# Gated-conv / GLA hybrid step: the small levels' scores in blocks of 32 tokens on the diagonal

## The reference, cut to what matters

```python
def gla_chunk(s, inp):
    q, k, v, gk = inp
    c = q.shape[2]
    b = jnp.cumsum(gk, axis=2)
    causal = jnp.tril(jnp.ones((c, c), dtype=bool))
    diff = b[:, :, :, None, :] - b[:, :, None, :, :]
    decay = jnp.exp(jnp.where(causal[None, None, :, :, None], diff, -jnp.inf))
    a = jnp.einsum('nhtd,nhsd,nhtsd->nhts', q, k, decay)
    o = jnp.einsum('nhts,nhsv->nhtv', a, v) + jnp.einsum('nhtd,nhdv->nhtv', q * jnp.exp(b), s)
```

## Time and profile before

| | us |
|---|---|
| median of 3 executions (lowest, highest) | 1970.84 (1970.3, 1971.75) |
| the profiled execution, device time | 1971.51 |
| its span, first to last instruction | 1969.7 |
| TensorE matmul busy | 1928.7 (98%) |
| TensorE weight load busy | 1863.0 |
| VectorE busy | 1086.9 |
| ScalarE busy | 814.3 |
| GpSimd busy | 360.0 |
| mean granted TensorE clock | 0.994 |

### The profile page before, as it was taken

How to read it: one execution, slowest core, us unless ns; L and a number is a source line. 1 busy time by engine, 2 the same in 40 slices (tenths; PEclk the granted TensorE clock), 3 DMA queues, 4 the chain that set the end, 5 groups by cost and what they waited for, 6 DMA issues and landing times. The chain is left out here.

```text
span 1969.7 us, 35737 instructions
## 1 busy us (share of the span) xinstructions
PE 1928.7 (98%) x14212; PEld 1863.0 (95%) x14212; DVE 1086.9 (55%) x1171; ACT 814.3 (41%) x1033; POOL 360.0 (18%) x423
## 2 busy tenths in 40 slices
PE   6999999999999999999999899999999999999997
PEld 5999889998899988999889899999999999999996
DVE  6556555565555655556565675444544454445555
ACT  5534445434454344543543353333333333333331
POOL 4241212312023120321200151000100010001400
PEclk9999999999999999999999899999999999999998
DMA  6645665557654476545744545555555555555542
GB/s 183 186 143 154 215 214 152 148 144 232 204 151 149 140 242 196 153 141 149 235 165 157 145 139 168 163 168 163 163 167 169 160 166 167 168 161 169 164 158 80
DMA packets 176152, 329.42 MB, mean 167 GB/s; under 512 B 11060, under 2 KB 29792, under 8 KB 175880
## 3 DMA queue, kind: packets, MB, share of 16 engines
q1 hardware_dynamic: 161016, 291.21, 49.4%
q10 hardware_dynamic: 9968, 19.16, 2.8%
q0 software_dynamic: 5072, 17.69, 2.8%
HBM read 306.59 MB, written 21.38 MB: 167 GB/s over the span
## 5 line engine op out<-in xcount | busy, mean ns | idle before, releaser
L351 DVE TENSOR_TENSOR w_lo<-raw,w_hi 128x1024 fp32r<-128x1024 f32 x544 | 724.4, 1335 | 798.0 <-ACT w_hi L346 797.8
L346 ACT ACTIVATE w_hi<-raw 128x1024 fp32r<-128x1024 f32 x544 | 574.7, 1058 | 919.0 <-PE bank L373 907.2
L371 PE MATMUL bank<-x_hi,w_hi 128*128 128x288 f32 (+2 forms) x3072 | 916.3, 298 | 5.1 <-DVE x_lo L397 2.9
L372 PE MATMUL bank<-x_lo,w_hi 128*128 128x288 f32 (+2 forms) x3072 | 910.7, 296 | 0.0
L373 PE MATMUL bank<-x_hi,w_lo 128*128 128x288 f32 (+2 forms) x3072 | 908.1, 296 | 0.0
L371 PEld LDWEIGHTS bank<-x_hi,w_hi 128*128 128x128 f32 x3072 | 578.0, 188 | 15.8 <-issue 11.2
L372 PEld LDWEIGHTS bank<-x_lo,w_hi 128*128 128x128 f32 x3072 | 578.1, 188 | 4.2 <-issue 2.9
L373 PEld LDWEIGHTS bank<-x_hi,w_lo 128*128 128x128 f32 x3072 | 577.4, 188 | 0.0
L373 PE MATMUL bank<-f_hi,w_lo 128*128 128x288 f32 x1280 | 379.5, 296 | 0.0
L371 PE MATMUL bank<-f_hi,w_hi 128*128 128x288 f32 x1280 | 378.9, 296 | 0.0
L372 PE MATMUL bank<-f_lo,w_hi 128*128 128x288 f32 x1280 | 373.2, 292 | 0.0
(11 more groups left out here) (238 smaller groups left out, 1044.1 us busy)
## 6 DMA issues: line engine op xcount, KB each, us to landing
raw<-in_w SPq DMA_DIRECT2D x256, 512.0 KB, 3.7
raw<-in_w_in SPq DMA_DIRECT2D x224, 512.0 KB, 3.7
out<-S ACTq DMA_DIRECT2D x36, 512.0 KB, 4.7
raw<-in_w_in SPq DMA_DIRECT2D x64, 256.0 KB, 3.1
S<-in_state_gla POOLq DMA_DIRECT2D x32, 512.0 KB, 6.6
raw<-in_w_o SPq DMA_DIRECT2D x32, 512.0 KB, 3.6
out<-yrow SPq DMA_DIRECT2D x8, 192.0 KB, 2.5
xrow<-in_x_prompt SPq DMA_DIRECT2D x2, 512.0 KB, 8.2
```

The lines of the kernel that those rows point to most:

```text
L346: nc.scalar.activation(w_hi[:, s, :, :], raw[:, s, :, :], ACT.Copy).then_inc(hi_ready, 1)
L351: nc.vector.tensor_tensor(w_lo[:, s, :, :], raw[:, s, :, :], w_hi[:, s, :, :].bitcast(F32), ALU.subtract).then_inc(lo_ready, 1)
L371: nc.tensor.matmul(out, wh, a_hi[:, kt, c0:c1], start=(kt == 0), stop=False)
L372: nc.tensor.matmul(out, wh, a_lo[:, kt, c0:c1], start=False, stop=False)
```

## The change

It adds `block_levels`, which takes the scores of the entries None, 1, 2, 4 and, after group 4, of level 8 only as 32x32 blocks on the diagonal of chunks 0 and 1. Block r of entry m lands in rows r to r+32, columns 32m to 32m+32 of the bank (level 8: columns r to r+32). VectorE's masked product and reduce then work on 128x128 instead of 128x512 elements and leave 128x32 sums in a corner of `att[:, 2]`, which four 32x32 additions put on the diagonal of `att` after the masked large levels, which are now written to `att` directly. The last 48 tokens and `large_levels` on TensorE are as before.

```diff
--- before.py
+++ after.py
@@ -51,6 +51,7 @@
 SLOTS = 4
 HG = 8
 CHUNK = 128
+BLOCK = 32
 CONV0 = META - (CW - 1)
 EARLY = 2 * CHUNK - META
 TT = 96
@@ -121,6 +122,7 @@
         scope.append(consts)
         mask = sb("mask", [P, 8, P], BF16)
         mask2 = sb("mask2", [P, 5, 48], BF16)
+        block_mask = sb("block_mask", [P, 4, BLOCK], BF16)
         segmask = sb("segmask", [P, NSEQ])
         carry = sb("carry", [P, T], BF16)
         a1T = sb("a1T", [RANK, T])
@@ -530,6 +532,18 @@
                         last = nc.tensor.matmul(out, ks, qs, start=(d == 0), stop=(d == DT - 1))
                 return last
 
+            def block_levels(h, c, entries, use, out):
+
+                pe.wait_ge(g_free[c], g_available(h, c, use))
+                for m, buf in enumerate(entries):
+                    for d in range(DT):
+                        for r in range(0, CHUNK, BLOCK):
+                            cols = slice(c * CHUNK + r, c * CHUNK + r + BLOCK)
+                            ks = QK[:, DT + d, cols] if buf is None else lev[:, buf, d, cols]
+                            qs = QK[:, d, cols] if buf is None else ks
+                            last = nc.tensor.matmul(out(m, r), ks, qs, start=(d == 0), stop=(d == DT - 1))
+                return last
+
             def large_levels(c):
 
                 for buf, L in enumerate(LEVELS[4:]):
@@ -626,7 +640,9 @@
                     if j == 2:
                         pe.wait_ge(lev_ready, 7 * h + 3)
                         for c in range(2):
-                            level(h, c, c, c * CHUNK, CHUNK, [None, 0, 1, 2], f"lev_a{c}").then_inc(g_full[c], 1)
+                            block_levels(h, c, [None, 0, 1, 2], f"lev_a{c}",
+                                         lambda m, r: gbank[c][r:r + BLOCK, m * BLOCK:(m + 1) * BLOCK])\
+                                .then_inc(g_full[c], 1)
                         level(h, 2, 2, 2 * CHUNK, 48, [None, 0, 1, 2], "lev_a2").then_inc(g_full[2], 1)
 
                         pe.wait_ge(qk_pool, 5 * h + 4)
@@ -653,7 +669,7 @@
                     if j == 4:
                         pe.wait_ge(lev_ready, 7 * h + 7)
                         for c in range(2):
-                            level(h, c, c, c * CHUNK, CHUNK, [3], f"lev_b{c}")
+                            block_levels(h, c, [3], f"lev_b{c}", lambda m, r: gbank[c][r:r + BLOCK, r:r + BLOCK])
                             large_levels(c).then_inc(g_full[c], 1)
                         level(h, 2, 2, 2 * CHUNK, 48, [3], "lev_b2")
                         for d in range(DT):
@@ -1089,16 +1105,20 @@
                 x = lev[:, lv, :, 0:hi]
                 return nc.vector.scalar_tensor_tensor(out=x, in0=x, scalar=-1.0, in1=x, op0=ALU.mult, op1=ALU.min)
 
-            def small_levels(h, k, use, w, msk):
+            def block_sums(c):
+
+                return att[:, 2, 64 + c * BLOCK:64 + (c + 1) * BLOCK]
+
+            def small_levels(h, k, use, rows, w, msk, sums):
 
                 if k > 0:
                     dve.wait_ge(sc1_ready, 3 * h + k)
                 dve.wait_ge(g_full[k], g_filled(h, k, use))
-                pr = prod[0:w, :, :].rearrange("p a b -> p (a b)")[:, 0:4 * w].rearrange("p (a b) -> p a b", b=w)
-                nc.vector.tensor_tensor(pr, gbank[k][0:w, 0:4 * w].rearrange("p (a b) -> p a b", b=w), msk, ALU.mult)\
+                pr = prod[0:rows, :, :].rearrange("p a b -> p (a b)")[:, 0:4 * w].rearrange("p (a b) -> p a b", b=w)
+                nc.vector.tensor_tensor(pr, gbank[k][0:rows, 0:4 * w].rearrange("p (a b) -> p a b", b=w), msk, ALU.mult)\
                     .then_inc(g_free[k], 1)
                 dve.wait_ge(g_free[k], g_emptied(h, k, use))
-                nc.vector.tensor_reduce(out=att[0:w, k, 0:w], in_=pr.rearrange("p a b -> p b a"), axis=AX_X, op=ALU.add)\
+                nc.vector.tensor_reduce(out=sums, in_=pr.rearrange("p a b -> p b a"), axis=AX_X, op=ALU.add)\
                     .then_inc(sc1_ready, 1)
 
             def large_levels(h, c):
@@ -1106,10 +1126,13 @@
                 if c > 0:
                     dve.wait_ge(att_ready, 3 * h + c)
                 dve.wait_ge(g_full[c], g_filled(h, c, f"lev_b{c}"))
-                nc.vector.tensor_tensor(tmpA[:, :], gbank[c][:, 0:CHUNK], mask[:, 4, :], ALU.mult).then_inc(g_free[c], 1)
+                nc.vector.tensor_tensor(att[:, c, :], gbank[c][:, 0:CHUNK], mask[:, 4, :], ALU.mult).then_inc(g_free[c], 1)
                 dve.wait_ge(g_free[c], g_emptied(h, c, f"lev_b{c}"))
                 dve.wait_ge(sc1_ready, 3 * h + 3)
-                nc.vector.tensor_tensor(att[:, c, :], att[:, c, :], tmpA[:, :], ALU.add).then_inc(att_ready, 1)
+                for r in range(0, CHUNK, BLOCK):
+                    a = att[r:r + BLOCK, c, r:r + BLOCK]
+                    last = nc.vector.tensor_tensor(a, a, block_sums(c)[r:r + BLOCK, :], ALU.add)
+                last.then_inc(att_ready, 1)
 
             def state_lo(h, i):
                 dve.wait_ge(s_hi_ready, NSEQ * h + i + 1)
@@ -1264,8 +1287,8 @@
                     if j == 2:
                         dve.wait_ge(masks_ready, 1)
                         for c in range(2):
-                            small_levels(h, c, f"lev_a{c}", CHUNK, mask[:, 0:4, :])
-                        small_levels(h, 2, "lev_a2", 48, mask2[0:48, 0:4, :])
+                            small_levels(h, c, f"lev_a{c}", P, BLOCK, block_mask[:, :, :], block_sums(c))
+                        small_levels(h, 2, "lev_a2", 48, 48, mask2[0:48, 0:4, :], att[0:48, 2, 0:48])
                     if j == 4:
                         for c in range(2):
                             large_levels(h, c)
@@ -1541,7 +1564,9 @@
                                                pattern=[[2 * L, P // (2 * L)], [0, L]], channel_multiplier=-1)
             seq(last)
             seq(nc.gpsimd.tensor_copy(mask2[0:48, :, :], mask[0:48, 0:5, 0:48]))
-            nc.gpsimd.memset(mask2[0:48, 3:5, META:48], 0.0)
+            seq(nc.gpsimd.memset(mask2[0:48, 3:5, META:48], 0.0))
+            for r in range(0, P, BLOCK):
+                seq(nc.gpsimd.tensor_copy(block_mask[r:r + BLOCK, :, :], mask[r:r + BLOCK, 0:4, r:r + BLOCK]))
 
             seq(nc.gpsimd.tensor_tensor(mask[:, 4, :], mask[:, 4, :], mask[:, 5, :], ALU.add))
             seq(nc.gpsimd.tensor_tensor(mask[:, 6, :], mask[:, 6, :], mask[:, 7, :], ALU.add))
```

## The result

| | before | after |
|---|---|---|
| median of 5 executions each, us | 1970.84 (1969.83 to 1972.17) | 1961.62 (1960.29 to 1963.78) |
| the profiled execution, us | 1971.51 | 1961.05 |

The ratio is 0.9946, 95% interval 0.9935 to 0.9957: 9.2 us or 0.5% less. Forecast were 1958.4, a range of 1956.0 to 1965.0, and a chance of 0.89 for faster by more than 0.2%.

The account below looks back on a forecast made before the run. TensorE was taken as the bound. A head would cost 0.30 + 160 x 0.009 = 1.74 us instead of 4.84, 3.10 less; four heads 12.4, so 1970.84 - 12.4 = 1958.4 us, range 1956.0 to 1965.0.

Parts of the forecast that it names:

- The bound: TensorE bounds the kernel, its matmuls busy 1928.7 of 1969.7 us; the other engines run ahead of it.
- the sum: On TensorE after groups 2 and 4, a head costs 1.74 us instead of 4.84: 3.10 less, 12.4 in four heads.
- 9 from 7 and 15: Price in ns of a 32-column record on TensorE: 9 taken, from 7 on four quarters and 15 on two.
- A change of form: TensorE switching between record shapes: 0.10 us each, two more after group 2, one after group 4, 0.30 us a head.
- The leads of the other engines: VectorE, GpSimd and the `w_lo` splits stay ahead of TensorE: cost 0, at most the 3.1 us saved per head.
- The reduce: VectorE's reduce after group 2 falls from 1.04 us to about 0.35, in proportion to its input.
- the additions: On VectorE after group 4, one addition of 0.29 us becomes four of 32x32, at most 0.27 each; cost 0.
- GpSimd's four copies: Four more mask copies on GpSimd, with five more waits: 2 us at most, at 46.8; cost 0.
- half the overlap: Rival: on TensorE only neighbouring records overlap, 15 ns a record, so 1962.2 us; chance 0.2.
- a part of the saving waited away: Rival: TensorE loses part of its saving to waits, most likely for `w_lo` in group 3: 1961 to 1966 us; chance 0.07.
- No overlap: Rival: short records on TensorE take 28 ns each, gaining 0.06 us a head, 1970.6 us, no change; chance 0.06.
- The rival on the slower side: Instructions don't come fast enough for 128 short records on TensorE: at 55 ns each, +17.0 us, 1987.9; chance 0.05.

Follow-up runs that it names:

- the experiment: Changed kernel with a 128x384 product and a reduce to 128x128 added on VectorE behind each chunk's small levels: 1962.64 us in one execution.
- the three kernels with 160 or more short records in a row: Changed kernel with four entries doubled (256 records): 1981.89 us; two doubled (192): 1970.45 us; last 48 tokens in blocks too, level 64 last, `onT` moved (160): 0.9942.

## Why the prediction was right, and where it was off

**The bound, the sum.** TensorE was the bound, and the timeline gave the sum: 1.34 us for the forecast 0.20 + 128 x 0.009 = 1.35 after group 2; 3.07 us a head for 3.10. The two parts of it hold apart as well. 64 records take 0.55 us from the first start to the last (117.16 to 117.71), 8.75 ns each, where I took 9 from 7 and 15. Those two I had read from the ends of the rows. By the starts, from which a cost on TensorE is to be read, the same records are 8 and 13 ns apart (0.105 us for 13 steps, 0.13 for the next 10); 9 lies between them all the same. A change of form costs about 0.1 us, as taken.

**The leads of the other engines.** They held: group 3 is 27.36 after 27.35, no wait for `w_lo` was added. The reduce took 0.40 for 0.35, the additions 0.25 each for at most 0.27, GpSimd's four copies 2.2 us for at most 2; all cost nothing, and for VectorE the experiment shows it in groups 2 to 4.

**What was left out** is chance. The difference of the medians was 9.2, the timeline's 12.3. I had read TensorE's waits as a list of small items and taken the rest of a head for unchanged, where groups 6 and 7 hold between 280 and 285 us from one execution to the next, in group 7 for a load's landing that stands in ScalarE's queue ahead of what TensorE needs. My range held it only because it reached to half the overlap and to a part of the saving waited away, neither of which happened: that 1961.62 lies within it is in part luck. 0.8 us for the spread of the runs was too little; a comparison of five executions each leaves some 2 us on either side.

**The rivals.** Half the overlap came out beside the measured time (1962.2), and the trace refutes it: 8.75 ns, not 15. No overlap is what the order of the loops decides, 27 ns in the one order and 8.75 in the other, and at 27 ns the result is no change that a single execution shows, as worked out (1972.06 beside 1972.76). The Trainium skill (TensorE: Matmul & The Clock Gate, on the 56 ns step) states a floor of 25 ns. The records of one quarter (27 ns) and of two halves (29 to 31) stay above it; those of four quarters in turn, at 8.75, do not. The rival on the slower side was right about its mechanism: the instructions do run dry, from 160 records in a row on. I had priced it at 55 ns a record and placed it in the queue between sequencer and array. It is a stop of 0.2 to 3.3 us at one place in every 256 instructions, in every head of the three kernels with 160 or more short records in a row, and behind five of the twelve stops the clock was at its lower level. At 128 records the changed kernel has none. The closest that two such places come in its profile is 5.1 us (head 3, 833.34 to 838.46). In eleven of the twelve heads that stopped, TensorE went on 4.0 to 4.5 us after the place before, and the stop was part of that time. No row of the trace before could show this.

## What to carry to other kernels

Small matmuls of 32 weight columns are worth their number only if neighbours in the program go to different quarters of the array: put the quarter in the innermost loop, and price them from a row of the trace that uses the same number of quarters. Count the instructions too: a stretch of short records that uses up a block of 256 instructions faster than the next one comes stops TensorE, and saving more work there makes the kernel slower. And before an effect of half a percent is explained, compare group by group along the timeline: what repeats to 0.01 us is the edit, what varies between heads is a wait of its own, which may be worth mending first.

## What the runs showed of the hardware

- Records for four quarters ran at 8.75 ns each, for two halves at 29 to 31, for one quarter, sixteen in a row, at 27; a change between these forms cost about 0.1 us.
- With four records in a row to a quarter the overlap stayed (10 ns), with sixteen it was gone.
- TensorE stopped for want of instructions in twelve places of three kernels, four in each, for 0.2 to 3.3 us, at intervals that are multiples of 256 of its instructions within a kernel. Each stop ended 2.2 to 2.8 us after the start of an instruction packet; the packets were 3.5 us apart at the closest, in kernels with stops and without. How many blocks it holds ahead, no run shows.
- After five of these twelve stops, all of them of 2.7 us or more, the granted clock was at the 1.2 GHz level for some 3 us while TensorE worked again; after two others as long, of 2.9 and 3.0 us, it stayed at 2.4 GHz. Why, no run tells.
